# A decoder layer on one core: every engine's order remade from later landing times

## The chip, the cores and the metric

The kernel runs on one core of one Trainium2 chip. The metric is device time in microseconds (us) of one launch. TensorE (PE), VectorE (DVE), ScalarE (ACT), GpSimd (POOL) and SyncE (SP) each carry out their own list of instructions in order and wait for each other by semaphores.

## The reference

One inference step of one decoder layer, in float32, width 1024. It has two streams of tokens: a prompt of 512 positions, and 8 decoding sequences with one new token each and 4096 cached positions.

```python
h = _rms(x, g_pre)
z = h @ w_in                      # 1024 -> 7 x 512
ua, va, ga, qb, kb, vb, gb = split(z)
ya = gelu(ua) * (tril(W_s) @ rms_group(gelu(va)) + b_s)
yb = attend(qb, kb, vb)           # 8 heads of 64
ya = _rms(ya) * silu(ga);  yb = _rms(yb) * silu(gb)
return x + _rms(concat(ya, yb) @ w_out, g_post)
```

`attend` is block-sparse attention with blocks of 256 positions. A query sees its own block and the 3 past blocks with the highest product of query and mean key; a linear distance penalty is added. For the prompt (two blocks) this is plain causal attention. For a decoding sequence it needs the sums of all 16 cached key blocks (32 pages of 128 rows, found through a page table), then the keys and values of 3 selected blocks per head.

## The kernel before, in words

**Prompt.** The input projection goes through seven chunks of 512 columns, in the order k, q, v, u, va, ga, gb (`CHUNKS`), each over four tiles of 128 positions. A tile is the step `("pj", c, t)`: 8 products of 128 x 128 by 128 x 512 (L1101), cut into four quarters so that shorter steps fit between them. The trace shows two matmuls for each such product, 4 for a quarter. The output projection is the same with steps `op` (L1210), two halves of four tiles. The weights of a chunk are 2 MB and come in one transfer (L825, step `wl`) into one of two buffers `wbuf`, asked for when the last tile of the chunk two before is done; only the first chunk's four quarters and the second chunk (L783) are loaded ahead of the planned order.

**Decoding.** The 8 new tokens go through the same weights, one step `("spj", c)` per chunk (L1044, 64 matmuls). The caches go one sequence ("batch") b at a time. GpSimd loads 16 key blocks with an indirect DMA each (`load_k`, L931, steps `ld`), at most `AHEAD` = 5 in flight and `SLOTS` = 18 in memory, so that the third block of a batch waits until the selected keys of the batch before have been read (steps `ex`, L757). VectorE adds the two halves of each block (steps `ks`, `sum_rows`, L744). PE sums them, four blocks a step (steps `gs`, groups 0 to 3, L1226). VectorE multiplies by q and picks the blocks (step `ga`, L1634 to L1658), turns them into pages (`pg`) and multiplies the selected keys by q (`ex`, `sr`). Small steps on PE and VectorE with one shared PSUM bank DC (`bc`, `mt`, `mb`, L1695 to L1715) make the softmax, and PE multiplies by the values (steps `pv0` and `pv1`, L1257), which SyncE, GpSimd and, in the last batch, ScalarE fetch with 32 KB transfers (`fetch_v`, L728).

**The start.** For each prompt tile, `("xn", t)` transposes it on PE (L1073) into two PSUM banks, which VectorE empties into `hT` (L1497). Three such banks serve all small steps of PE in turn.

**What sets the order.** Nothing is decided on the chip. When the program is built, `make_plan` runs a list scheduler over the six lanes PE, ACT, DVE, POOL, SP and Q. Each step has a length and the steps that it depends on; each engine has a few lanes by priority, a lane's own order is fixed, and the engine takes the step that can start first by the planned clock, by priority where several can. The lists that come out (`PLAN`) are the engines' programs. The waits of a step are the same wherever it stands. Since an engine carries out its list strictly in order, a step whose wait isn't met holds up everything behind it.

Q is no engine. It stands for the DMA queues as a planner's account: a key load takes `KEY_US` there, a value fetch (eight 32 KB transfers) `VALUE_US`, a weight block 7.0, one after the other (lanes value, key, weight), and it starts at `PLAN_START["Q"]`. After a transfer's turn on Q a further time passes until the planner counts it as landed:

```python
clock[eng] = start + lasts
ends[eng, s] = clock[eng] + (0.0 if eng != "Q" else 2.5 if s[0] == "v" else 0.8)
```

`LANDED` holds the planned landing of the first x tiles, the first chunk's weights and the second chunk's weights.

Of the kernel before, what the change touches and what calls it, by code (L numbers as in the profile page):

```python
# [9 lines left out]
ACT = mybir.ActivationFunctionType  # L10
# [38 lines left out]
def v_queue(b, k):  # L49

    if b < B - 1:
        return "POOL" if k == TOP - 1 else "SP"
    return ("SP", "POOL", "ACT")[k]


def make_plan():
# [9 lines left out]
    def add(eng, name, s, lasts, *deps):  # L66
        lanes[eng, name].append(s)
        spans[eng, s] = lasts
        needs[eng, s] = deps
# [7 lines left out]
    def project(s, lasts, *deps):  # L77
        add("PE", "project", s, lasts, *deps)
# [26 lines left out]
    def kt(t):  # L105
        add("PE", "side", ("kt", t), 0.5, ("ACT", ("pj", 0, t)))
        add("ACT", "side", ("kt", t), 0.6, ("PE", ("kt", t)))

    def sg(t):
        add("PE", "side", ("sg", t), 1.4, ("DVE", ("pj", 4, t)))  # L110
        add("DVE", "groups", ("sg", t), 1.3, ("PE", ("sg", t)))
# [13 lines left out]
    for c in range(len(CHUNKS)):  # L125
        spj(c)
        name = CHUNKS[c]
        for t in range(NT):
            first = [("Q", ("w", c))] if c else [("DVE", ("xn", t))]
            for x in range(QUARTERS):  # L130
                s = ("pj", c, t) if x == last else ("pj0", c, t, x)
                landed = [("Q", ("w0", x))] if (c, t) == (0, 0) else []
                if t == NT - 1 and x == 0:
                    landed.append(("PE", ("spj", c)))
                project(s, TILE_US / QUARTERS, *(first if x == 0 else []), *landed)
            deps = [("PE", ("pj", c, t))]
            lasts = 0.6
            if name == "va":
                lasts = 2.6
                if t >= 2:  # L140
                    deps.append(("PE", ("sg", t - 2)))
            if name in ("ga", "gb"):
                lasts = 1.5
                deps.append(("DVE", ("sg", t)) if name == "ga" else ("DVE", ("turn", PAIRS - 1)))
                if name == "ga":
                    deps.append(("DVE", ("pj", c, t - 2)) if t >= 2 else ("PE", ("sg", NT - 2 + t)))
                else:
                    deps.append(("DVE", ("pj", c - 1, t)) if t >= 2 else ("PE", ("sg", NT - 1)))
            if c == 0:
                deps.append(("POOL", ("xn", t)))  # L150
            if name == "q":
                add("DVE", "norm", ("pj", c, t), 0.7, *deps, ("ACT", ("rr",)))
            else:
                add("ACT", "evacuate", ("pj", c, t), lasts, *deps)
            if name == "k":
                add("SP", "rows", ("krow", t), 0.5, ("ACT", ("pj", c, t)))
            if name == "v":
                add("SP", "rows", ("vrow", t), 0.5, ("ACT", ("pj", c, t)))
            if name in ("va", "ga", "gb"):
                add("POOL", "root", ("pj", c, t), 1.3 if name == "va" else 0.9, ("ACT", ("pj", c, t)))  # L160
                add("DVE", "groups" if name == "va" else "scale", ("pj", c, t), 1.5 if name == "va" else 0.9,
                    ("POOL", ("pj", c, t)))
            if t == NT - 1 and c + 2 < len(CHUNKS) + 2:
                add("SP", "weights", ("wl", c + 2), 0.8, ("PE", ("pj", c, t)), ("Q", ("k", LOAD_BEHIND[c + 2], NB - 1)))
                add("Q", "weight", ("w", c + 2), 7.0, ("SP", ("wl", c + 2)))
            if name == "k" and t >= 1:
                kt(t - 1)
            if name == "va" and t >= 1:
                sg(t - 1)
            if (c, t) == (0, 3):  # L170
                add("DVE", "norm", ("rr",), 0.8, ("POOL", ("xn", NT - 1)))
                project(("rr",), 0.9, ("DVE", ("rr",)))
                add("ACT", "side", ("rr",), 0.6, ("PE", ("rr",)))
            if (c, t) == (1, 0):
                add("PE", "sample", ("sn",), 0.3, ("DVE", ("spj", 1)))
                add("DVE", "sample", ("sn",), 0.2, ("PE", ("sn",)))
            if (c, t) == (1, 3):
                project(("wt",), 0.5, ("POOL", ("const",)))
                add("DVE", "sample", ("wt",), 0.7, ("PE", ("wt",)))
        if name == "k":  # L180
            kt(NT - 1)
        if name == "va":
            sg(NT - 1)
# [25 lines left out]
    for a in range(len(pairs) + 2):  # L209
        if a >= 2:  # L210
            p, i = pairs[a - 2]
            s = ("pv", p, i)
# [6 lines left out]
        if 1 <= a <= len(pairs):  # L219
            p, i = pairs[a - 1]  # L220
            for hh in range(2):
                s = ("ptr", p, i, hh)
# [3 lines left out]
        if a < len(pairs):  # L226
            p, i = pairs[a]
            s = ("qk", p, i)
# [8 lines left out]
    for b in range(B):  # L237
# [44 lines left out]
        for hh in range(2):  # L282
            free = [("PE", (f"pv{hh}", b - 1))] if b else []
            landed.append([])
            for k in range(TOP):
                eng = v_queue(b, k)
# [5 lines left out]
        for hh in range(2):  # L292
            s = (f"pv{hh}", b)
# [31 lines left out]
    def bank(s):  # L325
        kind = s[0]
        if kind in ("pj0", "op0") and s[3] == 0:
            return "pa", 2, (("DVE" if kind == "op0" or s[1] == 1 else "ACT"), (kind[:-1],) + s[1:3])
        if kind in ("xn", "xs", "rr", "wt", "kt", "sg", "qk", "ptr", "turn", "yt", "spj", "fina", "fopa", "fin2", "fop"):
            freed = "DVE" if kind in ("xn", "xs", "wt", "sg", "qk", "turn", "yt", "fina", "fin2", "fop") else "ACT"  # L330
            return "sb", 3, (freed, ("fin2b",) if kind == "fin2" else s)
        if kind in ("rs", "ra", "bc", "mt", "mb", "pv0", "pv1", "sn", "fin0", "fin1", "ffd"):
            if kind in ("pv0", "pv1"):
                return "dc", 1, (("ACT", s) if s[1] < B - 1 else ("DVE", ("acc", int(kind[2]))))
            freed = "DVE"
            return "dc", 1, (freed, {"fin0": ("fin0b",), "ffd": ("ffd", 0)}.get(kind, s))
        return None

    clock = dict(PLAN_START)
    ends, plan = {}, {eng: [] for eng, _ in lanes}  # L340
# [5 lines left out]
    while True:  # L346
        best = None
        for x, line in lanes.items():
            if heads[x] == len(line):
                continue  # L350
            eng, s = x[0], line[heads[x]]
            deps = list(needs[eng, s])
            if eng == "PE" and bank(s):
                kind, size, _ = bank(s)
                held = 2 if s[0] in ("qk", "xn") else 1
                for back in range(size - held + 1, size + 1):
                    if len(banks[kind]) >= back:
                        deps.append(banks[kind][-back])
            if any(d not in ends for d in deps):
                continue  # L360
            ready = max([ends[d] + (0.0 if d[0] == eng else LAG) for d in deps] + [0.0])
            start = max(clock[eng], ready + (reach.get(x[1], 0.0) if eng == "PE" else 0.0))
            key = (start if start > clock[eng] + SLACK else clock[eng], rank[x], start)
            if best is None or key < best[0]:
                best = key, x, s, max(clock[eng], ready)
        if best is None:
            break
        _, x, s, start = best
        eng = x[0]
        lasts = spans[eng, s]  # L370
        if eng == "ACT":
            fn = {"qk": "exp", "fin0": "exp"}.get(s[0], table)
            if s[0] == "mb":
                fn = "exp"
            if s[0] in ("pj", "spj"):
                fn = {"u": "gelu", "va": "gelu", "ga": "silu", "gb": "silu"}.get(CHUNKS[s[1]], table)
            lasts += 1.3 * (fn != table)
            table = fn
        if eng == "PE" and bank(s):
            freed = [("DVE", s + (0,)), ("DVE", s + (1,))] if s[0] == "qk" else [bank(s)[2]] * (2 if s[0] == "xn" else 1)  # L380
            banks[bank(s)[0]].extend(freed)
        clock[eng] = start + lasts
        ends[eng, s] = clock[eng] + (0.0 if eng != "Q" else 2.5 if s[0] == "v" else 0.8)
        plan[eng].append(s)
        heads[x] += 1
    left = {x: line[heads[x]] for x, line in lanes.items() if heads[x] < len(line)}
# [2 lines left out]

PLAN_START = {"PE": 4.5, "ACT": 3.5, "DVE": 1.0, "POOL": 8.4, "SP": 20.0, "Q": 12.0}
LANDED = [(("x", 0), 4.3), (("x", 1), 10.5), (("x", 2), 13.0), (("x", 3), 14.5), (("xs",), 6.2), (("w", 1), 26.0),
          (("w0", 0), 6.8), (("w0", 1), 8.6), (("w0", 2), 10.4), (("w0", 3), 12.0)]
TILE_US, KEY_US, VALUE_US, LAG, MARGIN, SLACK, QUARTERS = 7.2, 1.65, 1.8, 0.25, 0.3, 0.05, 4
DVE_LANES = "attention groups norm out scale gate sample score tail"
POOL_LANES = "extract root tiny load fetch"

# [1417 lines left out]
```

## Time and profile before

| what | us |
|---|---|
| runs of the kernel, median (lowest to highest of 3) | 422.52 (419.89 to 427.89) |
| the profiled execution, its own time | 421.29 |
| its span, first to last instruction | 419.5 |
| PE busy in the span | 390.1 |
| VectorE, ScalarE, GpSimd busy | 263.2, 124.8, 278.5 |
| mean granted clock of TensorE | 0.985 of full |

The profiled execution lies within the runs, 1.2 us under their median. The span leaves out 1.8 us around the first and the last instruction. DMA moves 111.22 MB.

### The profile page before, as it was taken

The page shows a single profiled execution, that of the slowest core. Times are in us where ns is not written, and L with a number is a line of the kernel's source. Part 1 is how long each engine was busy: PE and PEld are TensorE (multiplying, and loading weights), DVE is VectorE, ACT ScalarE, POOL GpSimd, SP SyncE. Part 2 cuts the span into 40 slices and gives each one's busy share as a digit, 9 for nine tenths or more (in the row PEclk, how much of TensorE's full clock was granted, in tenths as well). Part 3 has the DMA queues.
Part 4 walks back from the last instruction along what each step waited for, and adds up shares of the span by engine and source line. Part 5 has one row for each costly group of instructions (what it writes and reads, how often), then busy time and mean ns, then how long its engine had stood idle before and what let it go on. Part 6 is the DMA issues. An engine that isn't in the chain of part 4 may idle for free.

```text
span 419.5 us, 9227 instructions
## 1 busy us (share of the span) xinstructions
PE 390.1 (93%) x2790; PEld 183.9 (44%) x2790; DVE 263.2 (63%) x695; ACT 124.8 (30%) x279; POOL 278.5 (66%) x438
## 2 busy tenths in 40 slices
PE   7779996999999999999879999999898899989994
PEld 4534354334533454444534546345332454344451
DVE  1165495446944696459746996579656865694532
ACT  4211110000121436446634357546242012011020
POOL 6867764484668766757878777688768856675011
PEclk9999998999999999999989999999999899999998
DMA  8999389999599899977998199975999999925121
GB/s 274 368 395 375 123 268 381 336 287 284 198 352 361 189 354 345 333 185 270 292 316 241 34 367 344 308 155 155 337 367 328 318 380 397 198 63 108 67 99 53
DMA packets 78599, 111.22 MB, mean 265 GB/s; under 512 B 45744, under 2 KB 46896, under 8 KB 78552
## 3 DMA queue, kind: packets, MB, share of 16 engines
q0 software_dynamic: 22576, 71.45, 50.7%
q1 hardware_dynamic: 51992, 36.79, 31.3%
q10 hardware_dynamic: 3984, 2.41, 1.9%
q8 instruction: 22, 0.36, 0.4%
q14 instruction: 25, 0.20, 0.2%
HBM read 106.31 MB, written 4.29 MB: 264 GB/s over the span
## 4 chain that ended last, share of the span: by engine, by line
PE 18%; SPq 14%; DMA 7%; issue 7%; DVE 4%; POOL 3%; DVEq 1%; POOLq 0%; ACT 0%; ACTq 0%
PE PA L1210 14%; SPq L728 11%; DMA K<-in_cache_k,kidx 3%; DMA wbuf<-in_w_out 3%; DVE ksum L757 2%; DMA V<-in_cache_v 2%; POOL K L931 1%; SPq L724 1%; PE GB L1226 1%; PE SB L1044 1%; SPq L726 1%; PE SB L1196 1%; PE DC L1257 1%; POOL rstd L950 1%; POOL ksum L757 0%
## 5 line engine op out<-in xcount | busy, mean ns | idle before, releaser
L1101 PE MATMUL PA<-wbuf,hT 128*128 128x512 f32 x384 | 181.7, 611 | 1.2 <-DMA wbuf<-in_w_in 1.0
L931 POOL DMA_INDIRECT K<-in_cache_k,kidx x128 | 134.2, 1049 | 69.2 <-issue 36.4
L744 DVE TENSOR_TENSOR ksum<-K 128x512 f32<-128x512 f32 x128 | 86.2, 690 | 59.1 <-DMA K<-in_cache_k,kidx 52.6
L1101 PEld LDWEIGHTS PA<-wbuf,hT 128*128 128x128 f32 x384 | 69.2, 193 | 76.8 <-issue 74.2
L728 POOL DMA_DIRECT2D V<-in_cache_v x128 | 76.4, 599 | 16.8 <-issue 11.0
L1210 PE MATMUL PA<-wbuf,hT 128*128 128x512 f32 x128 | 59.2, 604 | 0.1
L757 DVE TENSOR_TENSOR ksum<-K,qb 128x128 f32<-128x128 f32 x128 | 41.1, 394 | 1.6 <-DVE selT L1658 1.3
L757 POOL TENSOR_TENSOR ksum<-K,qb 128x128 f32<-128x128 f32 x64 | 30.4, 507 | 12.2 <-DVE selT L1658 11.1
L1226 PE MATMUL GB<-ksum,win 128*32 128x512 f32 x256 | 34.1, 604 | 4.8 <-DVE ksum L744 4.8
L1210 PEld LDWEIGHTS PA<-wbuf,hT 128*128 128x128 f32 x128 | 22.9, 189 | 25.7 <-issue 25.2
L1101 PE MATMUL PA<-hT,wbuf 128*128 128x512 f32 x64 | 29.0, 599 | 0.0
L1690 DVE TENSOR_REDUCE sc<-ksum 128x48 f32<-128x3072 f32 x8 | 26.6, 3327 | 0.0
L1044 PE MATMUL SB<-wbuf,hTs 128*32 128x128 f32 x576 | 19.3, 289 | 6.3 <-DMA wbuf<-in_w_in 6.1
L1393 ACT ACTIVATE pr<-pr,smin 128x128 f32<-128x128 f32 (+3 forms) x32 | 17.7, 555 | 22.9 <-DVE smin L1580 22.8
L1359 ACT ACT_TABLE_LOAD x13 | 16.7, 1283 | 21.8 <-PE PA L1101 21.7
L947 POOL TENSOR_TENSOR rstd<-msum,nhalf 128x1 f32<-128x1 f32 x6 | 3.3, 550 | 27.6 <-DVE msum L1612 14.7
L1044 PEld LDWEIGHTS SB<-wbuf,hTs 128*32 128x32 f32 x576 | 16.4, 116 | 10.3 <-DMA wbuf<-in_w_in 5.0
L1402 ACT COPY pT<-SB 128x128 f32<-128x128 f32 (+3 forms) x32 | 12.6, 427 | 23.3 <-PE SB L1164 21.9
L1101 PEld LDWEIGHTS PA<-hT,wbuf 128*128 128x128 f32 x64 | 11.6, 190 | 13.7 <-issue 13.6
L1580 DVE CUSTOM_DVE_ANT_0 pr<-alibi,SB 128x128 f32<-128x128 f32 (+3 forms) x32 | 14.3, 484 | 4.4 <-PE SB L1155 4.3
L1257 PE MATMUL DC<-V,pex 128*32 128x64 f32 x768 | 13.9, 220 | 3.2 <-DMA V<-in_cache_v 3.2
L1305 ACT ACTIVATE junk<-PA 128x512 bf16<-128x512 f32 x8 | 4.8, 598 | 39.7 <-PE PA L1210 39.7
(226 smaller groups left out, 371.9 us busy)
## 6 DMA issues: line engine op xcount, KB each, us to landing
wbuf<-in_w_in SPq DMA_DIRECT2D x6, 2048.0 KB, 10.8
V<-in_cache_v SPq DMA_DIRECT2D x240, 32.0 KB
V<-in_cache_v POOLq DMA_DIRECT2D x128, 32.0 KB, 6.4
wbuf<-in_w_out SPq DMA_DIRECT2D x2, 2048.0 KB, 21.6
wbuf<-in_w_in SPq DMA_DIRECT2D x4, 512.0 KB, 10.3
K<-in_cache_k,kidx POOLq DMA_INDIRECT x128, 8.0
qb<-q_rows SPq DMA_DIRECT2D x8, 256.0 KB
v<-in_x_prompt ACTq DMA_DIRECT2D x2, 512.0 KB, 9.6
```

The source lines that it names most:

```text
L728: eng.dma_start(V[j * ROWS:(j + 1) * ROWS, x * TOP + k, :, :], v_pages[bass.ds(page, 1), :, :, HEAD[x] * HD:(HEAD[x] + 1) * HD] .rearrange ...
L744: eng.tensor_tensor(ksum[:, n % SUMS, :], K[:, at, 0, :], K[:, at, 1, :], ALU.add).then_inc(s_dsum, 1)
L757: last = eng.tensor_tensor(kq[:, x * TOP + k, :, :], K[:, bass.ds(n, 1), :, col:col + HD].rearrange("p a r d -> p (a r) d"), qb[:, col:col ...
L931: pool.indirect_dma_start(K[:, m % SLOTS, :, :].rearrange("p r w -> p (r w)"), None, k_rows, bass.IndirectOffsetOnAxis(ap=kidx[:, b, n:n + ...
L1044: last = pe.matmul(bank[32 * j:32 * j + 32, 0:P], src[:, kc, :], w[:, kc, j * P:(j + 1) * P], start=(kc == kcs[0]), stop=(kc == kcs[-1]), ...
L1101: last = pe.matmul(bank[:, :], lhs, rhs, start=(kc == 0), stop=(kc == KC - 1))
L1210: last = pe.matmul(bank[:, :], hT[:, kc, t * P:(t + 1) * P], wbuf[:, c % 2, kc, :], start=(kc == 0), stop=(kc == KC - 1))
L1226: last = pe.matmul(GB[32 * j:32 * j + 32, :], win[:, 31 - g:63 - g], ksum[:, (4 * g + j) % SUMS, :], start=(g == 0), stop=(g == G - 1), ti ...
L1257: last = pe.matmul(DC[32 * j:32 * j + 32, hh * HD:(hh + 1) * HD], pex[:, h, i, r:r + 1].broadcast_to([P, 32]), V[:, h * TOP + i, r, :], st ...
L1359: act.activation(dst, bank, fn, scale=sc_).then_inc(pa_free[n % 2], 1)
L1393: act.activation(pr[:, hh, 0:(i + 1) * P], pr[:, hh, 0:(i + 1) * P], ACT.Exp, bias=smin[:, hh:hh + 1], scale=-1.0, accum_out=ssum[:, 2 * p ...
L1690: dve.tensor_reduce(sc[:, :, :, :].rearrange("p h k r -> p (h k) r"), kq[:, :, :, :], AX.X, ALU.add).then_inc(s_scr, 1)
```

## The change

Five numbers of the planner's account of DMA change, and nothing else:

- a key or weight counts as landed 2.8 us after its turn on Q, where it was 0.8 us; values 4.0 us, where it was 2.5;
- a weight's turn takes 8.0 us, where it was 7.0 (`wl` and its transfer stay);
- a key's turn takes 1.5 us, where it was 1.65;
- Q starts at 14.0 us, where it was 12.0.

The program is built from the lists that `make_plan` gives with these numbers, so on each engine the same steps with the same instructions stand in another order. PSUM banks and semaphore counts are assigned along the order and follow it.

```diff
--- before.py
+++ after.py
@@ -162,7 +162,7 @@
                     ("POOL", ("pj", c, t)))
             if t == NT - 1 and c + 2 < len(CHUNKS) + 2:
                 add("SP", "weights", ("wl", c + 2), 0.8, ("PE", ("pj", c, t)), ("Q", ("k", LOAD_BEHIND[c + 2], NB - 1)))
-                add("Q", "weight", ("w", c + 2), 7.0, ("SP", ("wl", c + 2)))
+                add("Q", "weight", ("w", c + 2), 8.0, ("SP", ("wl", c + 2)))
             if name == "k" and t >= 1:
                 kt(t - 1)
             if name == "va" and t >= 1:
@@ -380,7 +380,7 @@
             freed = [("DVE", s + (0,)), ("DVE", s + (1,))] if s[0] == "qk" else [bank(s)[2]] * (2 if s[0] == "xn" else 1)
             banks[bank(s)[0]].extend(freed)
         clock[eng] = start + lasts
-        ends[eng, s] = clock[eng] + (0.0 if eng != "Q" else 2.5 if s[0] == "v" else 0.8)
+        ends[eng, s] = clock[eng] + (0.0 if eng != "Q" else 4.0 if s[0] == "v" else 2.8)
         plan[eng].append(s)
         heads[x] += 1
     left = {x: line[heads[x]] for x, line in lanes.items() if heads[x] < len(line)}
@@ -389,10 +389,10 @@
 
 
 
-PLAN_START = {"PE": 4.5, "ACT": 3.5, "DVE": 1.0, "POOL": 8.4, "SP": 20.0, "Q": 12.0}
+PLAN_START = {"PE": 4.5, "ACT": 3.5, "DVE": 1.0, "POOL": 8.4, "SP": 20.0, "Q": 14.0}
 LANDED = [(("x", 0), 4.3), (("x", 1), 10.5), (("x", 2), 13.0), (("x", 3), 14.5), (("xs",), 6.2), (("w", 1), 26.0),
           (("w0", 0), 6.8), (("w0", 1), 8.6), (("w0", 2), 10.4), (("w0", 3), 12.0)]
-TILE_US, KEY_US, VALUE_US, LAG, MARGIN, SLACK, QUARTERS = 7.2, 1.65, 1.8, 0.25, 0.3, 0.05, 4
+TILE_US, KEY_US, VALUE_US, LAG, MARGIN, SLACK, QUARTERS = 7.2, 1.5, 1.8, 0.25, 0.3, 0.05, 4
 DVE_LANES = "attention groups norm out scale gate sample score tail"
 POOL_LANES = "extract root tiny load fetch"
```

## Rows read from the trace of the kernel before

**Rows 1.** The page: span, busy time by engine, granted clock by slice

```profile
span 419.5 us, 9227 instructions
...
PE 390.1 (93%) x2790; PEld 183.9 (44%) x2790; DVE 263.2 (63%) x695; ACT 124.8 (30%) x279; POOL 278.5 (66%) x438
...
PEclk9999998999999999999989999999999899999998
```

**Rows 2.** PE's waits: line, what ended them, us in total, times, longest

```profile
PE SB L1044 <- DMA wbuf<-in_w_in: 6.1, 3, 3.5
PE GB L1226 <- DVE ksum L744: 4.8, 4, 1.7
PE DC L1257 <- DMA V<-in_cache_v: 3.2, 2, 2.5
```

**Rows 3.** The last value product and matmuls; SyncE's value issues

```profile
400.89 0.81 PE DC L1257 x48
...
409.91 3.64 PE PA L1210 x8
...
L728 SPq DMA_DIRECT2D V<-in_cache_v x240: 537/537/3889, 61.2 to 389.0; - x120
```

**Rows 4.** Timeline at `spj`: start us, us, instruction, idle before it

```profile
15.97 1.96 PE L1044 MATMUL SB<-wbuf,hTs 128*32 128x128 f32 x64 [2.03 <-DMA wbuf<-in_w_in]
...
58.21 0.39 SPq L825 DMA_DIRECT2D wbuf<-in_w_in  x1
...
69.08 3.43 PE L1044 MATMUL SB<-wbuf,hTs 128*32 128x128 f32 x64 [3.48 <-DMA wbuf<-in_w_in]
```

**Rows 5.** Landing of weights, keys and values; key loads in one stretch

```profile
DMA to landing us min/median/max: 5.8/11.0/21.6
...
DMA to landing us min/median/max: 4.3/8.0/11.3
...
DMA to landing us min/median/max: 2.0/6.4/9.7
...
115.00:129.00 14.00, 8.39 (x9) 1.00 1.06 361
```

**Rows 6.** Timeline of 23 to 28 us, VectorE and PE

```profile
23.24 0.69 DVE L744 TENSOR_TENSOR ksum<-K 128x512 f32<-128x512 f32 x1 [5.15 <-DMA K<-in_cache_k,kidx]
...
23.85 1.28 DVE L1497 TENSOR_TENSOR hT<-SB,gpre 128x512 f32<-128x512 f32 x2
24.59 0.42 PEld L1073 LDWEIGHTS SB<-ident,v 128*128 128x128 f32 x4 [2.01 <-DVE hT L1497]
...
28.11 0.16 PEld L1226 LDWEIGHTS GB<-ksum,win 128*32 128x32 f32 x8 [1.98 <-DVE ksum L744]
```

**Rows 7.** Timeline at PE's later waits; clock of one stretch

```profile
209.46 1.06 PE L1226 MATMUL GB<-ksum,win 128*32 128x512 f32 x8 [1.10 <-DVE ksum L744]
...
281.32 0.88 PE L1257 MATMUL DC<-V,pex 128*32 128x64 f32 x48 [0.73 <-DMA V<-in_cache_v]
...
301.51 1.07 PE L1226 MATMUL GB<-ksum,win 128*32 128x512 f32 x8 [1.71 <-DVE ksum L744]
...
317.79 1.06 PE L1226 MATMUL GB<-ksum,win 128*32 128x512 f32 x8 [0.85 <-DVE ksum L744]
...
326.71 0.88 PE L1257 MATMUL DC<-V,pex 128*32 128x64 f32 x48 [2.50 <-DMA V<-in_cache_v]
...
373.51 0.21 PE L1251 MATMUL DC<-psm,one 128*32 128x2 f32 x5 [2.04 <-issue]
...
323.00:337.00 14.00, 11.31 (x148) 5.58 (x149) 12.12 (x29) 2.52 (x8) 10.98 (x18) 0.88 1.13 307
```

**Rows 8.** Timeline of 214 to 215 us, VectorE and PE

```profile
214.18 0.69 DVE L744 TENSOR_TENSOR ksum<-K 128x512 f32<-128x512 f32 x1 [2.21 <-DMA K<-in_cache_k,kidx]
214.79 0.20 DVE L1715 TENSOR_TENSOR sc<-sc,DC 128x48 f32<-128x48 f32 x1
...
215.04 0.16 PEld L1055 LDWEIGHTS DC<-msum,fold 128*32 128x32 f32 x8 [2.95 <-DVE sc L1715]
```

## The prediction

> **What bounds the kernel now.** I read the page first [rows 1]: TensorE (PE) is busy for 390.1 us of a span of 419.5 us, 93%, and the line of the granted clock is at full nearly everywhere. No other engine comes near (the page gives GpSimd 66%, VectorE 63%, ScalarE 30%). The change adds no instruction and takes none away, so those 390 us stay. What an order can alter is the rest: 419.5 - 390.1 = 29.4 us in which PE does nothing, and what half clock costs after such a pause.
>
> Then the waits of PE [rows 2] and the timeline at each of them say where the 29.4 us lie. 1.6 us are ahead of the first matmul and 6.0 us behind the last one (413.54 to 419.54 [rows 3]), where ScalarE and VectorE finish the last tile; neither can move. Another 3.2 us are waits for the first weights, the largest 2.03 at 15.97 [rows 4]; their landing times stand in `LANDED`, which stays as it is. There remain 18.5 us in the middle, and nearly all of them are one kind: an engine stands, by its fixed order, at a step whose transfer (key, value or weight) has not landed, while other work is ready behind it. The planner believed that it had.
>
> What it believed is read off its constants: after the planner's queue is done with a transfer, a key is there 0.8 us later, a weight 7.0 + 0.8 = 7.8 us after it is asked for, a value 2.5 us after the queue. The trace has a weight block issued at 58.21 and used the moment it lands, at 69.08: 10.9 us [rows 4]. All weights: 5.8 to 21.6 us, median 11.0 [rows 5]. Keys take 4.3 to 11.3 us, median 8.0, and values 2.0 to 9.7, median 6.4 [rows 5].
>
> **The change, part by part.** Every price below is an idle time in the profiled execution.
>
> Weights: 8.0 + 2.8 = 10.8 us instead of 7.8, almost exactly the 10.9 measured. The sample step of the third chunk (`spj 2`, L1044) then stands some 3 us later in PE's order, behind one or two quarters of a projection tile (4 matmuls, 1.9 us each), whose weights are there. Its wait of 3.48 us goes, and with it what followed: the clock fell to its lower level (1.2 GHz) and the 64 matmuls took 3.43 us where the same 64 took 1.96 at 16 us [rows 4], 1.47 us more. Together 4.95; I take 4.5, bounds 0 and 5.0. The block is asked for once the tile before it is done, so a step that moves later can't find it later still. PE's three waits at this step sum to 6.1 us [rows 2]: with 2.03 and 3.48 that leaves 0.6 for the fifth block, which goes the same way. The output projection's blocks take up to 21.6 us, but PE waits 0.2 us for them in all: nothing.
>
> First keys: the queue starts at 14 instead of 12 us and a key lands 2.8 us after it, so the first one comes at about 14 + 1.5 + 2.8 = 18.3 us for the planner, where it had 14.5 (VectorE first sums one at 17.33). VectorE stood at the second key from 18.1 to 23.24 us and only then emptied the banks of `xn 2`, for which PE waited 1.77 us, to 24.59 [rows 6]. With the second key planned at 19.8 instead of 16.1, emptying `xn 2` (its transposes end at 19 us) comes first. The 1.77 goes; I take 1.7, bounds 0 and 1.8, since the third key can now stand ahead of `xn 3` in the same way. The first group sum waits 1.15 us at 28.11 [rows 6]; planned later by a quarter of a tile, 1.0 of it goes (bounds +1 and -1.15).
>
> Later keys: 2.0 us of latency more, but 1.5 instead of 1.65 us each. For the sixth key behind a selection (group 1 needs it last) that is 2.0 - 6 x 0.15 = 1.1 us later, for the fourteenth 2.0 - 14 x 0.15 = 0.1 us earlier. So group 1 is helped and group 3 is not: of the waits at 209.46 (1.10) and 301.51 (1.71) [rows 7] 1.1 each go, of the 0.85 at 317.79 nothing. The trace has nine key loads in 14 us, 1.56 each [rows 5]: 1.5 is nearly right.
>
> Values: 4.0 instead of 2.5 us, 1.5 later. Of the waits of the value products at 281.3 (0.73), 326.71 (2.50) and 373.51 (2.04; the row says issue, but the step waits for values) [rows 7] go 0.7, 1.5 and 1.5. The clock was at half for part of 323 to 337 (mean 0.88 [rows 7]): 0.12 x 14 = 1.7 us of full clock lost, part of which returns. Later keys and values together: 1.1 + 1.1 + 3.7 = 5.9, with 1 for the clock 6.9; since steps move by whole quarters and the later orders are all remade, I take 5, bounds 0 and 10.6 (the six waits, 8.9 us, and the clock).
>
> Not hit: at 215.04 PE waits 2.12 us because VectorE stands at a key sum until 214.18 and only then does the short step `mb` (L1715) that frees the bank [rows 8]. Whether a key sum again stands ahead of a short step can't be read from the constants. I take 0, bounds -3.8 (the wait and the lower clock behind it) and +3.8.
>
> What comes new: queues are remade everywhere. VectorE, ScalarE, GpSimd and SyncE each get steps in other places; every key load (1.0 us of issue on GpSimd), every value issue (0.54 us on SyncE) and store behind a moved step moves with it. A group sum placed later delays the selection of its batch, and with it the next loads; two quarters, 3.8 us, is the most that one shift of 2 to 3 us does. The 18.5 us in the middle are a dozen waits, 1.6 us each. I take three new ones of that size, 5 us, bounds 0 and 15.
>
> Sum: -4.5 - 0.6 - 1.7 - 1.0 - 5 + 5 = -7.8 us. From the profiled execution's own 421.3 us (span 419.5 and 1.8 around it) that is 413.5; from the median of the runs, 422.5, it is 414.7. I say 414.
>
> Will the decode chain let PE run ahead? The gain before 80 us (about 7 us) doesn't wait for keys: the selections follow group sums that PE itself does late, so they move up too. At the end the last value product is over at 401.7, with 12 us of PE work behind it, and SyncE issues its last value at 389.0. With the median landing that is 395.4, the product starts at 400.89 [rows 3]: 5.5 us of slack, enough for what the late half gains in the forecast, not for much more.
>
> On the pause and the clock the Trainium skill says, in "TensorE: Matmul & The Clock Gate" (Terms), that the penalty is the throttled time times (1 - K/N), half of it at the lower level. The trace agrees roughly: 1.47 us lost over 3.43 us [rows 4].
>
> **Rivals.** (1) The waits only change places. For: a key takes anything from 4.3 to 11.3 us and a weight up to 21.6, so one constant is wrong for many of them whatever it is, and the seven or so waits behind 150 us come from different causes (keys, values, a VectorE queue). Against: the early ones are plain misjudgements of 3 to 5 us. Then 7.8 us go early, 6 or more come back: about 420. The Trainium skill has it so in "DMA: Bandwidth & Descriptors" (Latency and other measured facts): HBM access is 0.2 us on average and 2 us at high load, so a fixed addition fits only the loaded stretches.
>
> (2) Slower: the planner's queue becomes too fast for the chip. Per batch it holds 16 keys, 6 values and a weight: 16 x 1.65 + 6 x 1.8 + 7 = 44.2 us before, 16 x 1.5 + 10.8 + 8 = 42.8 after. Where the queue paces the plan, batches come 1.4 us sooner each, and from the third on this outweighs the 2.0 us of latency; group sums 2 and 3 then stand ahead of their keys. Price: a wait of about 2.1 us and the clock behind it, 1.7, in each of the five last batches, 19 us, less the 7.8 gained early: about 432. Against: in the trace one kind of batch step alone, key loads in a row, runs at 1.56 us; and behind the fourth batch the pace is set by attention and selections rather than by the queue.
>
> (3) All of it works: every wait in the middle but two goes, with the clock: 18.5 - 3.5 = 15 us and some 3 us of clock: about 404. Against: the slack at the end is 5.5 us.
>
> **How the numbers follow.** Forecast 0.50 (its own range 409 to 419), rival 1 0.22 (417 to 424), rival 2 0.10 (425 to 436), rival 3 0.18 (402 to 409). A measurement of this kernel tells 2% from no change, 8.5 us: its runs lie between 419.9 and 427.9. Faster by over 2% (under 414.0): rival 3 and half of the forecast, 0.42. Slower (over 431): 0.07. Within: 0.51. The range for 8 in 10 is 406 to 424: it leaves out rival 2 and the lower half of rival 3.
>
> **What would show it.** Right: PE busy 385 to 390 us; no wait above 1 us at `spj 2`, whose 64 matmuls take 1.96 us; no wait for L1497 near 24 us; VectorE empties `xn 2` ahead of the second key; PE's idle time near 20 us instead of 29.4; two or fewer stretches at half clock. Wrong: a key sum ahead of its key holds VectorE for more than 3 us while PE is idle; waits at L1226 for the later groups of batches 3 to 7; PE idle between the last value product and the end.

## The result, and the profile after

| what | before | after |
|---|---|---|
| runs, median (lowest to highest), us | 421.2 (418.9 to 427.9, 4 runs) | 429.5 (426.4 to 431.1, 4 runs) |
| ratio, with its 95% interval | | 1.024 [1.017, 1.031] |
| profiled execution, own time / span, us | 421.3 / 419.5 | 426.4 / 424.3 |
| PE busy / granted clock | 390.1 / 0.985 | 392.5 / 0.975 |

The changed kernel is 2.4% slower, where I had forecast 414 us, 7.8 us faster. Its profiled execution is the fastest of its four, so the profile shows some 5 us of the 8.

The page after, the lines that answer to [rows 1]:

```profile
span 424.3 us, 9225 instructions
...
PE 392.5 (92%) x2790; PEld 185.3 (44%) x2790; DVE 260.7 (61%) x695; ACT 124.5 (29%) x279; POOL 282.7 (67%) x438
...
PEclk9996999999999999999999989999998899999998
```

PE is idle for 31.8 us (29.4 before), and the work itself took 2.4 us longer, with more of it at the lower clock. The waits of PE after, which answer to [rows 2]:

```profile
PE GB L1226 <- DVE ksum L744: 9.6, 6, 4.4
PE SB L1044 <- DMA wbuf<-in_w_in: 5.6, 2, 3.8
PE DC L1242 <- DVE dgm L1712: 1.7, 1, 1.7
PE DC L1238 <- DVE mx L1704: 1.7, 2, 1.4
...
PE SB L1196 <- DVE hT L1601: 1.0, 1, 1.0
```

The waits for keys (through the sums at L744) have doubled, from 4.8 to 9.6 us. Waits for values, 3.2 us before, are gone from the list. New are waits for VectorE's small steps (L1242, L1238, L1196).

**The first 40 us.** The timeline after, VectorE first, answers to [rows 6]:

```profile
18.97 1.29 DVE L1497 TENSOR_TENSOR hT<-SB,gpre 128x512 f32<-128x512 f32 x2 [3.64 <-PE SB L1073]
...
20.98 1.30 DVE L744 TENSOR_TENSOR ksum<-K 128x512 f32<-128x512 f32 x2
```

The same view of after, PE at its longest wait in this stretch:

```profile
32.35 3.64 PE L1044 MATMUL SB<-wbuf,hTs 128*32 128x128 f32 x64 [3.78 <-DMA wbuf<-in_w_in]
```

VectorE empties the banks of `xn 2` at 18.97 and sums keys from 20.98 on, as predicted; PE's wait for it is gone. But PE, early now, stands at the second chunk's sample step (`spj 1`, L1044) at 28.57, whose weights land at 32.35: 3.78 us of waiting, and the 64 matmuls took 3.64 us at 1.2 GHz instead of 1.96. How much of this wait belongs to the order and how much to this one execution is seen under e3. The stretches of after with a lower clock, columns as in the last row of [rows 7]:

```profile
28.00:40.00 12.00, 8.22 (x79) 4.84 (x72) 4.72 (x9) 0.37 (x1) 8.50 (x9) 0.72 1.06 379
247.00:259.00 12.00, 8.61 (x46) 4.42 (x46) 6.42 (x18) 3.54 (x8) 6.84 (x8) 0.86 1.07 362
296.00:333.00 37.00, 29.02 (x105) 11.63 (x104) 18.77 (x48) 7.29 (x16) 26.95 (x37) 0.91 1.06 337
320.00:333.00 13.00, 8.63 (x20) 2.94 (x19) 6.68 (x22) 1.30 (x3) 8.97 (x16) 0.74 1.13 289
```

The kernel before in the two stretches that start at 247 and 296 us:

```profile
247.00:259.00 12.00, 11.70 (x133) 7.14 (x133) 9.32 (x33) 9.74 (x16) 8.39 (x9) 1.00 1.01 345
296.00:333.00 37.00, 31.94 (x174) 13.72 (x174) 25.42 (x66) 9.86 (x17) 29.18 (x45) 0.95 1.08 332
```

In 12 us from 28 on the lower clock cost PE of the changed kernel 0.28 x 12 = 3.4 us of full clock; a part of it fell on the wait itself.

**From 236 us on.** The last projection tile of the fifth chunk in PE's order, `pj 4 3`, is done at 236.4 us in after and 239.5 in before: up to here the changed kernel was 3 us ahead in these two executions. From there to the last tile of the output projection it takes 180.9 us, before 174.0. The two worst places in the timeline after, the first from 246 to 258 us, VectorE and PE:

```profile
246.99 0.69 DVE L744 TENSOR_TENSOR ksum<-K 128x512 f32<-128x512 f32 x1
...
249.03 0.69 DVE L744 TENSOR_TENSOR ksum<-K 128x512 f32<-128x512 f32 x1 [1.35 <-DMA K<-in_cache_k,kidx]
...
249.78 1.91 PE L1226 MATMUL GB<-ksum,win 128*32 128x512 f32 x8 [1.57 <-DVE ksum L744]
...
251.08 0.69 DVE L744 TENSOR_TENSOR ksum<-K 128x512 f32<-128x512 f32 x1 [1.35 <-DMA K<-in_cache_k,kidx]
...
253.27 0.69 DVE L744 TENSOR_TENSOR ksum<-K 128x512 f32<-128x512 f32 x1 [1.50 <-DMA K<-in_cache_k,kidx]
253.88 0.68 DVE L1580 CUSTOM_DVE_ANT_0 pr<-alibi,SB 128x512 f32<-128x512 f32 x1
...
256.94 0.27 DVE L1709 TENSOR_REDUCE mrow<-DC 8x1 f32<-8x128 f32 x1
...
257.79 0.35 PE L1242 MATMUL DC<-dgm,one 8*128 8x8 f32 x2 [1.75 <-DVE dgm L1712]
```

The planner put four key sums of batch 5 in a row, ahead of attention's first product (L1580) and of `mt 4` (L1709). The last three each wait for their key, about 2 us apart. VectorE reaches `mt 4` at 256.94, and PE, which needs it for `mb 4` (L1242), has waited 1.75 us. Before, the same 12 us held 11.7 us of PE work against 8.6 now.

The second, in the round of batch 6, with SyncE's issues of the residual's loads, GpSimd's of key loads and PE's wait:

```profile
304.85 0.93 SPq L860 DMA_DIRECT2D qT<-in_x_prompt  x2
...
305.83 1.15 SPq L860 DMA_DIRECT2D kT<-in_x_prompt  x2
...
307.95 1.29 POOL L931 DMA_INDIRECT K<-in_cache_k,kidx  x1 [0.53 <-issue]
...
312.04 0.94 POOL L931 DMA_INDIRECT K<-in_cache_k,kidx  x1 [1.08 <-DMA K<-in_cache_k,kidx]
...
325.75 1.94 PE L1226 MATMUL GB<-ksum,win 128*32 128x512 f32 x8 [4.37 <-DVE ksum L744]
```

How long batch 6's key loads took to land, after:

```profile
DMA to landing us min/median/max: 5.9/10.2/12.9
```

The same of the kernel before, from 285 to 320 us:

```profile
DMA to landing us min/median/max: 5.8/8.1/10.7
```

SyncE issues the residual's loads (2.5 MB; its tiles take the place of qT and kT) at 304.85 us, as before (304.4). But the first key load of batch 6 behind the selection is issued at 291.3 us instead of 286.8, so that more of the batch's loads are issued behind the residual: the last at 312.04, landing 12.9 us later. Landing times in the two windows are 5.9 to 12.9 us, median 10.2, after, and 5.8 to 10.7, median 8.1, before. PE waits 4.37 us at the last group sum and then runs at the lower clock (mean 0.74 over 13 us). At the end PE's last instruction is a small step of the decode chain (L1055, over at 417.54) and not the last tile's matmul, and 6.8 us follow instead of 6.0. The chain that ends last is that of a tile of y in both kernels; after, the decode chain's last steps stand in it.

### The profile page after: what moved, and what is told of

Same layout as the page of the kernel before. It is cut to its first block and busy times, and to the rows that moved or that the text cites. A ratio compares the mean times of both kernels' runs of the same rounds, so it can differ in the third digit from the quotient of the medians.

```text
span 424.3 us, 9225 instructions
## 1 busy us (share of the span) xinstructions
PE 392.5 (92%) x2790; PEld 185.3 (44%) x2790; DVE 260.7 (61%) x695; ACT 124.5 (29%) x279; POOL 282.7 (67%) x438
## 5 line engine op out<-in xcount | busy, mean ns | idle before, releaser
L744 DVE TENSOR_TENSOR ksum<-K 128x512 f32<-128x512 f32 x128 | 85.4, 688 | 56.5 <-DMA K<-in_cache_k,kidx 47.2
L1226 PE MATMUL GB<-ksum,win 128*32 128x512 f32 x256 | 35.9, 632 | 9.6 <-DVE ksum L744 9.6
L757 POOL TENSOR_TENSOR ksum<-K,qb 128x128 f32<-128x128 f32 x64 | 33.9, 561 | 9.7 <-issue 4.9
L757 DVE TENSOR_TENSOR ksum<-K,qb 128x128 f32<-128x128 f32 x128 | 37.8, 368 | 3.2 <-DVE selT L1658 2.9
L1044 PE MATMUL SB<-wbuf,hTs 128*32 128x128 f32 x576 | 19.5, 290 | 5.6 <-DMA wbuf<-in_w_in 5.6
L1044 PEld LDWEIGHTS SB<-wbuf,hTs 128*32 128x32 f32 x576 | 16.4, 116 | 10.3 <-DMA wbuf<-in_w_in 5.4
L1580 DVE CUSTOM_DVE_ANT_0 pr<-alibi,SB 128x128 f32<-128x128 f32 (+3 forms) x32 | 14.3, 482 | 9.7 <-PE SB L1155 9.7
L1226 PEld LDWEIGHTS GB<-ksum,win 128*32 128x32 f32 x256 | 5.2, 109 | 27.4 <-DVE ksum L744 16.6
```

Of the source, the lines that this page charges most:

```text
L744: eng.tensor_tensor(ksum[:, n % SUMS, :], K[:, at, 0, :], K[:, at, 1, :], ALU.add).then_inc(s_dsum, 1)
L757: last = eng.tensor_tensor(kq[:, x * TOP + k, :, :], K[:, bass.ds(n, 1), :, col:col + HD].rearrange("p a r d -> p (a r) d"), qb[:, col:col ...
L1044: last = pe.matmul(bank[32 * j:32 * j + 32, 0:P], src[:, kc, :], w[:, kc, j * P:(j + 1) * P], start=(kc == kcs[0]), stop=(kc == kcs[-1]), ...
L1226: last = pe.matmul(GB[32 * j:32 * j + 32, :], win[:, 31 - g:63 - g], ksum[:, (4 * g + j) % SUMS, :], start=(g == 0), stop=(g == G - 1), ti ...
L1580: last = dve.tensor_tensor_reduce(out=pr[:, hh, 0:m], in0=alibi[:, SEQ - m:SEQ], in1=sb_bank(s)[:, 0:m], scale=-SLOPES[2 * p + hh], scalar ...
```

## The experiments

The first four ask which part of the order carries the loss, and whether named waits do. Ratios are to the kernel before on the same chip, with 95% intervals. Line numbers in profiles of these kernels are shifted by the lines added.

**e1 and e2: new landing times for one half.**

```diff
+        early = s[1] < {"k": 5, "v": 4, "w": 6}[s[0]]
+        new = early            # e2: not early
+        lasts = {"k": 1.5 if new else 1.65, "v": VALUE_US, "w": 8.0 if new else 7.0}[s[0]]
...
+        ... (4.0 if new else 2.5) if s[0] == "v" else 2.8 if new else 0.8
```

> The new numbers for the keys of batches 0 to 4, values of 0 to 3 and weights of chunks 2 to 5, the old ones for everything later; PE's order is the changed kernel's up to 245 us of the planner's clock. Theory 'late half': the changed kernel was 3.7 us ahead of the kernel before at 243 us and lost 8 us or more behind that, so this one is about as fast as before or faster: 415 to 421 us, with its waits behind 247 us no longer than before's. Rival 'early half' (the first-weights wait of 3.8 us and 7 us of half clock decide, or the early orders harm the late ones): 425 to 430 us.

> The reverse: old numbers for batches 0 to 4 (values 0 to 3, chunks 2 to 5), new ones later; PE's order is the kernel before's up to 250 us of the planner's clock. Theory 'late half': the new numbers make the order of the last batches worse, 425 to 431 us, with long waits at L1226 or in the last value products behind 295 us. Rival 'early half': 419 to 423 us, as before.

e1: 425.4 us, 1.011 [0.993, 1.028], 4 runs. e2: 421.2 us, 1.001 [0.994, 1.007], 10 runs. The new numbers for the second half alone give no loss. For e1 the runs can't tell: its interval holds no loss and the whole loss. Its trace has the loss, 180.9 us from `pj 4 3` to the last tile as after, and the long waits behind 245 us (2.38 at 249, 4.79 at 318 us), with the old numbers in force there: the planner's state at 236 us is another, and so is everything it plans behind. e2's order up to 245 us is that of before. Both theories had looked for the fault in the numbers of one half; this pair doesn't tell where it sits in the order.

**e3: the second chunk's weights planned at 32 us.**

```diff
-(("w", 1), 26.0)
+(("w", 1), 32.0)
```

> The changed kernel with one more number: the second chunk's weights are planned to land at 32 us, not at 26; only the orders of the first 50 us differ. Theory: the wait of 3.78 us at 28.6 us (for weights that land at 32.3 us) and the half clock from 31.4 to 38.2 us (3.4 us lost) go, and PE is 5 to 7 us ahead at 60 us; the total falls by 2 to 6 us against the changed kernel (424 to 427 of 429.5), less if the last batches are paced by keys. Rival: the late waits eat it whole, 428 to 431 us.

428.4 us, 1.018 [1.001, 1.035]. The wait and its half clock are gone, and `pj 0 3` is done at 53.9 us instead of 58.9. Of that, 2.2 us are left at 236 us and 1.9 at the last tile. The total is 1 us under the changed kernel's, less than these runs can tell. Nor can the early gain be put down to e3: in e4, e10, e14 and e15, whose orders are the changed kernel's up to here, `pj 0 3` is done at 53.3 us too, and PE waited at most 0.99 us at `spj 1`. This is e14 there (L1057 is L1044):

```profile
29.58 1.63 PE L1057 MATMUL SB<-wbuf,hTs 128*32 128x128 f32 x52 [0.99 <-DMA wbuf<-in_w_in]
```

The second chunk's weights took 18.3 us to land in the profile of after (asked for at 14.05), and 14.8, 15.3 and 14.9 us in e10, e14 and e15. Over all eight profiled executions with this early order the wait was 0, 0.19, 0.22, 0.99, 1.61, 2.65, 3.72 and 3.78 us. So the new order waits for these weights, 1.6 us on the mean (before's order, in four executions, never did), and the 3.78 us are the most seen, not its usual size.

**e4: three steps of VectorE moved.**

```diff
+    for s in (("mt", 4), ("qk", 2, 3, 1), ("qk", 2, 3, 0)):
+        line.remove(s)
+        line.insert(line.index(("ks", 5, 3)) + 1, s)
```

> The changed kernel with three steps of VectorE moved by hand: qk (2,3) in both halves and mt 4 stand ahead of the key sums 4 and 5 of batch 5, where they stood behind them. Theory: VectorE held by unlanded keys between 248 and 257 us cost PE 1.75 us at L1242 and the half clock; with the steps moved this wait is under 0.3 us and the first key load of batch 6 comes 1 to 3 us earlier than at 291.3; total 1 to 4 us under the changed kernel. Rival: the place doesn't matter, since batch 6's keys are late for another reason (the residual loads on the same DMA engines): wait gone, total within 1 us of the changed kernel.

428.2 us, 1.019 [1.000, 1.037]. The wait at L1242 is gone; PE now waits 2.31 us at 252.7 us for the bank that VectorE empties later (`sg 3`). The last part takes 179.4 us, 1.5 less than after. The first key load of batch 6 behind the selection is issued at 287.3 us, 4.0 earlier than after (2.5, counted from `pj 4 3`). But PE's wait for the last keys of batch 6 did not shrink with it (L1235 is L1226, L753 is L744):

```profile
300.89 0.94 SPq L869 DMA_DIRECT2D qT<-in_x_prompt  x2
...
321.91 1.61 PE L1235 MATMUL GB<-ksum,win 128*32 128x512 f32 x8 [4.70 <-DVE ksum L753]
```

The residual's loads (L869 is L860) moved ahead by the same 4.0 us, from 304.85 to 300.89, so that five key loads still followed them, as after; in the kernel before it was two.

**e5, e6, e7: tiny changes of the planner that say nothing of landing.**

```diff
-KEY_US = 1.65    # e5, in the kernel before
+KEY_US = 1.64
-LAG = 0.25       # e6, in the kernel before
+LAG = 0.27
-KEY_US = 1.5     # e7, in the changed kernel
+KEY_US = 1.51
```

> The kernel before with one key's turn at 1.64 instead of 1.65 us: a difference that says nothing of landing, yet 456 places of the five engines' orders hold another step (585 between before and after). Theory 'draw': any new order of this planner loses against the one before, which is a lucky one; expected 1 to 2.5% over before, 425 to 432 us. Rival 'landing times': the old landing times as such make the order good, so this stays within 0.7% of before, 420 to 425 us.

> The kernel before with the planner's time between engines at 0.27 instead of 0.25 us, 565 places changed, landing times as before. Theory 'draw': 425 to 432 us. Rival 'landing times': 420 to 425 us.

> The changed kernel with one key's turn at 1.51 instead of 1.50 us, 323 places changed. Theory 'draw': it can fall anywhere from 421 to 432 us. Rival 'landing times': 427 to 432 us, as the changed kernel.

e5: 422.6 us, 1.007 [1.002, 1.011]. e6: 432.4 us, 1.025 [1.014, 1.035]. e7: 426.4 us, 1.014 [1.007, 1.022]. A step of 0.02 us in a number that says nothing of landing cost as much as the whole change. e5 was on the rival's side, so "any new order loses 1% or more" is refuted as well; that the order is a draw fits all three, and three is few. What e6 drew shows in PE's waits:

```profile
PE SB L1044 <- DMA wbuf<-in_w_in: 7.9, 3, 4.1
PE SB L1044 <- DMA wbuf<-in_w_out: 7.7, 1, 7.7
PE GB L1226 <- DVE ksum L744: 5.1, 4, 3.2
```

Here the sample step of the output projection stands 7.7 us ahead of its weights, which before had been waited for 0.2 us.

**e9 and e10: the residual's loads cut to 128 of 1024 columns,** in before and in after.

```diff
-sp.dma_start(xres[t], x_rows[t]...)
+sp.dma_start(xres[t][:, 0:1, 0:128], x_rows[t]...[:, 0:1, 0:128])
-sp.dma_start(gpost, g_post.broadcast_to([P, D]))
+sp.dma_start(gpost[:, 0:128], g_post[:, 0:128].broadcast_to([P, 128]))
```

> The changed kernel with the residual's and the post-gain's loads (5 DMAs, 2.5 MB, issued at 305 us) cut to 128 of 1024 columns, so the residual added is mostly not loaded; the DMAs, waits and orders stay. Theory 'traffic': the last keys of batch 6, which took 12.9 us to land, come in 8 to 9 us, PE's wait of 4.37 us at L1226 falls under 1.5 us and the 6.8 us of half clock to 0 or 3.4; 5 to 7 us of 426 go. Rival 'late selection': the keys are late because their first load is issued 4.5 us late; the wait falls by under 1.5 us.

> The kernel before with the same cut. Theory 'traffic': its last keys of batch 6 land in 8 instead of 10 us and the wait of 2.50 us for values at 324 us shrinks; 1 to 4 us of 421 go, less than from the changed kernel. Rival: nothing moves by more than 1 us.

One execution each, so totals (425.1 and 426.3 us, beside 424.7 for before) say little; the stretches inside say more. Landing of batch 6's keys in e10, same window as above:

```profile
DMA to landing us min/median/max: 5.1/7.0/8.7
```

8.7 us at most instead of 12.9, and PE's wait for the last group is 0.52 us instead of 4.37. From the last group sum of batch 5 to that of batch 6 it takes 44.6 us instead of 49.0 (before: 43.4, e9: 42.8). But of these 4.4 us only 0.4 are left in the last part as a whole (180.5 us instead of 180.9): PE then waits 5.6 us between 328 and 347 us, for values and for small steps of VectorE. The traffic explains the wait, not the loss. "5 to 7 us go" was wrong.

**e11, e12, e13: two orders joined.** Up to a planned time each engine's steps stand in one kernel's order, behind it in the other's.

```diff
+    first, _ = make_plan(later_first)
+    rest, began = make_plan(not later_first)
+    for eng, line in rest.items():
+        done = {s for s in line if began[eng, s] < cut}
+        out[eng] = [s for s in first[eng] if s in done] + [s for s in line if s not in done]
```

> Two orders joined, word for word: on each engine the steps that the kernel before plans up to 236 us stand in the changed kernel's order, all later ones in the order of the kernel before. Theory 'late half': the first part of the changed order is a little faster than before's (pj(4,3) done at 234 to 239 us in five executions, against 235 to 246 in three), the last part of before's is 5 to 7 us faster than the changed one's (174 against 181 us from there to the last tile); so 416 to 421 us, at or below before. Rival 'the join or the state of the queues decides, not the order': 425 us or more.

> The mirror image: before's order up to 236 us, the changed kernel's from there. Theory 'late half': 426 to 433 us, the whole loss of the change and a little more, with the waits at L1226 behind 295 us and a tail of 6.8 us. Rival: under 424 us.

> The join e11 with the cut at 235 instead of 236 us, so that SyncE asks for the sixth weight block ahead of batch 5's q row, as in the kernel before; in e11 it stood behind, and PE waited 6.1 us for that block at 249 us, with 6.8 us of half clock behind. Theory 'late half': without this wait the last part takes 174 to 177 us as in before, and the total is 416 to 421 us, at or below before. Rival 'an order fits only its own history': 423 to 427 us again, with waits at other places.

| | first part | last part | median, us | ratio | `pj 4 3` done | from there to the last tile |
|---|---|---|---|---|---|---|
| before | before | before | | 1 | 239.5 | 174.0 |
| after | after | after | 429.5 | 1.024 [1.017, 1.031] | 236.4 | 180.9 |
| e12 | before | after | 430.0 | 1.021 [1.016, 1.025] | 232.8 | 185.0 |
| e11 | after | before | 424.8 | 1.005 [1.001, 1.010] | 236.7 | 182.5 |
| e13 | after | before | 418.5 | 0.992 [0.987, 0.996] | 236.6 | 177.0 |

The last two columns are of the profiled executions. e12 has the loss: the last part of the changed order costs 2%. e13 is 0.8% under before, but that doesn't show what the first part is worth: its join was picked after e11 had failed, and 0.8% is within what e5 to e7 move by changes that mean nothing. The traces have `pj 4 3` done at 234.1 to 239.1 us in eight executions with the changed kernel's first part (mean 236.4) and at 232.8 to 245.5 in four with before's (mean 238.2), 1.8 us on the mean, inside the scatter.

The lists of e11 and e13 differ in two places and no more: SyncE asks for the seventh chunk's weights (`wl 6`) behind batch 5's q row in e11, ahead of it in e13. The request came only 1.2 us later, at 237.88 instead of 236.65 us, but PE got the block only 17.1 us after its request, where in e13 it landed after 12.1, and waited 6.1 us for it, with 6.8 us of half clock. The two ratios lie apart by more than their intervals. In e13 no wait behind 236 us is longer than 2.4 us; PE's waits of e13:

```profile
PE GB L1240 <- DVE ksum L758: 4.4, 4, 2.2
...
PE DC L1271 <- DMA V<-in_cache_v: 2.4, 1, 2.4
PE DC L1265 <- issue: 2.1, 1, 2.1
```

(L1240 is L1226 of the kernel before, L1271 and L1265 are L1257 and L1251.) PE's waits of e12 against it:

```profile
PE GB L1240 <- DVE ksum L758: 11.1, 7, 3.5
PE DC L1256 <- DVE dgm L1726: 3.3, 1, 3.3
PE SB L1210 <- DVE hT L1615: 3.1, 1, 3.1
```

11.1 us for key sums against 4.4 in the whole run. e13 is the fastest version that I ran, and it beats both kernels.

**e14 and e15: the named places, in the changed kernel.** e14 moves the residual's loads, e15 these and e4's three steps.

```diff
+    line = plan["SP"]
+    line.remove(("res",))
+    line.insert(line.index(("wl", 7)), ("res",))
```

> The changed kernel with SyncE's step res (the residual's and the post-gain's loads, 2.5 MB) moved behind the values of batch 5, just ahead of the weight block of the output projection; nothing else moves. Theory 'traffic': the last keys of batch 6 land in 8 to 9 us instead of 12.9, the wait of 4.37 us at L1226 falls under 1.5 us, 2 to 4 us of 429 go. Rival: the loads then collide with the output weights or are late for the first tile of y, and the total stays at 428 to 432 us.

> The changed kernel with both: the residual's loads late (e14) and the three VectorE steps ahead of two key sums (e4). Theory 'two places': 421 to 425 us. Rival 'the whole order': 426 us or more, the waits having moved to the value products and to the first steps of the output projection (326 to 346 us).

e14: 427.8 us, 1.016 [1.009, 1.024]; its wait for the last keys of batch 6 is 0.47 us instead of 4.37. e15: 424.2 us, 1.011 [1.002, 1.019]. Each alone takes 1 to 2 us, which by itself isn't clear of the noise; with both the ratio is 1.011 instead of 1.024, about half of the loss, but the two intervals overlap. The traces show less: the last part takes 180.9 us in after, 179.4 in e4, 180.8 in e14 and 178.8 in e15, so that both together bring back 2.1 of 6.9 us. In e14 the wait for the keys is gone and the last part is as long as without the move: PE then waits 1.03 and 1.51 us for values at 333 and 339 us, and the wait for VectorE at 258 us, which lies ahead of the moved loads, was 3.24 us in this execution and 1.75 in that of after. And e15 still has 8.2 us of waits for key sums in nine places.

## Why the prediction was wrong

**What bounds the kernel:** right. PE's work stayed at 390 us, 2.4 more by the clock, and all that changed were waits and the clock behind them.

**Weights, -4.5 and -0.6:** the two waits are gone in the profiled execution, but in part by luck. At `spj 2` PE waited 0, 1.96, 3.48 and 7.42 us in the four profiled executions with before's order up to there, and 0, 0, 0.48, 0.84, 1.15, 1.84, 4.11 and 4.14 us in the eight with the changed one: 3.2 us on the mean against 1.6. The step was moved the right way, and about half of the term came.

**First keys, -1.7 and -1.0:** the two waits went as described. But the sum took them as gained. I had set the second chunk's weights aside because their entry in `LANDED` doesn't change; that PE, coming earlier, would stand before them, I didn't ask. It does, for 1.6 us on the mean and for 3.78 us, with 3.4 us of full clock behind it, in the profile of after. The four early terms summed to 7.8 us; at 236 us the traces have 1.8 us of gain on the mean (236.4 against 238.2).

**Not hit, 0:** the wait of 2.12 us at 215 us is gone, and one of the same kind, a short step of VectorE behind key sums, is new at 257.79 (1.75 us).

**Later keys and values, -5:** of the six waits (8.9 us) four went altogether, the three for values and the one at 209 us, more than I took. 1.71 became 1.40 and 0.85 became 4.37. By themselves the six shrank by 3.2 us. I treated each wait as a place that stays and gets the planned shift; in truth the whole list behind it is another one.

**New waits, +5:** here the forecast failed. I took three waits of 1.6 us, sized like the old ones, for the whole kernel, and nothing for the clock behind them. Behind 236 us alone PE has about 10 us of waiting that before didn't have: 0.42, 1.57, 1.75, 1.86 and 1.05 us in new places and 3.5 us more at the last keys of batch 6. With the waits that went, idle time there rose from 8.4 to 13.1 us. The lower clock lasted 10.2 us instead of 3.4, and PE's work took 2.4 us longer; the end behind PE's last instruction is 0.8 us longer. Together the kernel behind 236 us takes 187.9 us instead of 180.0, 7.9 us more, where the terms for that part had summed to zero. The upper bound that I wrote down for new waits, 15 us, was the right size for the doubt; the 5 was worked out from nothing but the size of the old ones.

**The chain of the last part** is only in part supported. The hold of VectorE by key sums at 247 to 257 us costs PE the wait at L1242 and delays batch 6's loads (e4 removes the one and brings the loads 4.0 us forward). The wait for batch 6's last keys comes from the residual's traffic (e10 and e14 remove it). That the first causes the second is not so in e4, where the loads came earlier, the residual's loads with them, and the wait stayed, at 4.70 us. Nor are these two places over half of the loss in the traces (e15: 2.1 of 6.9 us).

**The rivals.** Rival 1 (waits change places) is nearest to what happened, but more came back than had gone. Rival 2 gave the right size, 432 us, by a mechanism that is only half there: the third key loads of batches 2 to 5 are issued 1.0 to 3.2 us sooner, and waits for key sums doubled; but batches 6 and 7 come 4.5 and 7.9 us later, and the waits lie in batches 5 and 6 alone, not one in each of the last five. Rival 3 is refuted. What none of them said is what e5 to e7 show: changes that mean nothing move the kernel by up to 2.5%, more than the gain that I forecast. I gave "slower by over 2%" 0.07.

**The clock:** a pause costs more than I had it. At `spj 2` before I priced 1.47 us, the 64 matmuls' own loss; at `spj 1` after they lost 1.68 us (3.64 against 1.96), but the lower clock lasted 6.8 us, from 31.4 on, and cost 3.4 us of full clock in all. I had counted the clock only where it went away. The Trainium skill's rule ("TensorE: Matmul & The Clock Gate", Terms: the penalty is the throttled time times one minus the ratio) fits roughly: 3.64 us at the lower level, half of it 1.82, against 1.68 measured.

**Still open:** which property of before's last part makes it fast. Two other orders with the old numbers in force there (e1 and e6) took 180.9 and 183.4 us, one from the new numbers behind before's history (e2) 176.0. None of the five numbers was changed by itself, so which of them remade the last part isn't known either.

## What to carry to other kernels

A list scheduler's whole order hangs on each of its numbers. Better numbers can improve the places that they describe, but here the rest was drawn anew; before you judge a change of its model, measure a few meaningless changes of the same size (0.01 and 0.02 us here) and see how far they scatter. A wait that goes is a gain only as far as the next thing with a fixed time, so follow the engine to it. And a wait read from one profile may be that execution's alone: look at the same place in other executions of the same order before you price it. If part of a new order is better, join it to the old one and look for what the join itself delays.

## What the runs showed that I hadn't expected

The same order on the same chip differs by 1.5% from run to run (415.2 to 421.3 us for e13), and the profiled executions show one source: in four of them with before's order up to 236 us, `pj 4 3` is done at 232.8, 234.8, 239.5 and 245.5 us. The spread is in the third chunk's weights: PE waited for them 0, 1.96, 3.48 and 7.42 us at `spj 2`.
